# First column block of the first FFN: input x fetched in four pieces, first weights fetched and split by columns, in a fused two-layer decoder trunk on Trainium2

## What is computed

```
def swiglu(x, w_gate, w_up, w_down):
    return (jax.nn.silu(x @ w_gate) * (x @ w_up)) @ w_down
...
    for l in range(DEPTH):
        x = layer_norm(ALPHA * x + 0.5 * swiglu(x, ffn1_w_gate[l], ffn1_w_up[l], ffn1_w_down[l]),
                       ln1_g[l], ln1_b[l])
        mix = hybrid_mixer(x, w_in[l], ...)
        x = layer_norm(ALPHA * x + mix, ln2_g[l], ln2_b[l])
        x = layer_norm(ALPHA * x + 0.5 * swiglu(x, ffn2_w_gate[l], ffn2_w_up[l], ffn2_w_down[l]),
                       ln3_g[l], ln3_b[l])
```

## Time and profile before

| | |
|---|---|
| median of 3 runs | 1083.84 us (1083.62 to 1085.15) |
| the profiled execution's own time | 1083.67 us |
| its span, first to last instruction | 1081.9 us |
| PE busy | 1072.1 us, 99% of the span |
| PE weight loads busy | 882.7 us, 82% |
| DVE / ACT / GpSimd (POOL) busy | 772.0 / 579.4 / 137.3 us |
| mean DMA rate over the span | 209 GB/s |
| granted TensorE clock, mean | 0.999 |

### The profile page before, as it was taken

The page is one execution under the profiler, slowest core; times in us unless marked ns, Lnnn a source line. Parts: engine busy times, 40 slices in busy tenths (PEclk is TensorE's granted clock), DMA queues, the critical chain, the costliest instruction groups (busy, mean ns, idle before and its releaser), DMA issues.

```text
span 1081.9 us, 14282 instructions
## 1 busy us (share of the span) xinstructions
PE 1072.1 (99%) x5197; PEld 882.7 (82%) x5197; DVE 772.0 (71%) x779; ACT 579.4 (54%) x641; POOL 137.3 (13%) x137
## 2 busy tenths in 40 slices
PE   8999999999999999999999999999999999999997
PEld 6888888888888788888888888888878887888886
DVE  5756557799979775555679665677999787655566
ACT  5755654768554544444456655547774546344441
POOL 1498000000000000000006970000000000000000
PEclk9999999999999999999999999999999999999999
DMA  8877879355566486777737877775455674688761
GB/s 285 263 216 231 296 223 225 105 184 171 175 185 208 149 272 226 233 259 225 250 124 231 248 244 254 230 199 165 148 166 157 195 268 133 209 268 270 235 208 40
DMA packets 192371, 226.39 MB, mean 209 GB/s; under 512 B 31540, under 2 KB 157128, under 8 KB 192328
## 3 DMA queue, kind: packets, MB, share of 16 engines
q1 hardware_dynamic: 192328, 225.83, 65.5%
HBM read 214.26 MB, written 11.53 MB: 209 GB/s over the span
## 4 chain that ended last, share of the span: by engine, by line
PE 97%; DMA 1%; SPq 1%; DVE 1%; issue 0%; ACT 0%; DVEq 0%
PE ps L578 25%; PE ps L555 19%; PE ps L557 18%; PE ps L556 18%; PE ps L538 4%; PE ps L540 2%; PE ps L974 1%; PE ps L976 1%; PE ps L975 1%; PE ps L593 1%; DMA raw<-in_ffn_w_up 1%; PE ps L901 1%; DMA tp<-in_ln_b 0%; PE ps L686 0%; PE ps L685 0%; PE ps L684 0%
## 5 line engine op out<-in xcount | busy, mean ns | idle before, releaser
L1449 DVE TENSOR_TENSOR w_lo<-raw,w_hi 128x2048 fp32r<-128x2048 f32 x172 | 399.9, 2329 | 166.7 <-ACT w_hi L1058 165.6
L1058 ACT CAST w_hi<-raw 128x2048 fp32r<-128x2048 f32 x172 | 328.1, 1910 | 162.1 <-PE ps L578 78.9
L555 PE MATMUL ps<-w_hi,xT 128*128 128x512 f32 x848 | 331.8, 391 | 0.3 <-DVE w_lo L1461 0.2
L556 PE MATMUL ps<-w_lo,xT 128*128 128x512 f32 x848 | 330.1, 389 | 0.0
L557 PE MATMUL ps<-w_hi,xT 128*128 128x512 f32 x848 | 330.1, 389 | 0.0
L555 PEld LDWEIGHTS ps<-w_hi,xT 128*128 128x128 f32 x848 | 159.2, 188 | 36.2 <-issue 2.5
L557 PEld LDWEIGHTS ps<-w_hi,xT 128*128 128x128 f32 x848 | 159.2, 188 | 33.0
L556 PEld LDWEIGHTS ps<-w_lo,xT 128*128 128x128 f32 x848 | 159.2, 188 | 32.7
L578 PE MATMUL ps<-w_hi,rows_hi 128*128 128x512 f32 x396 | 126.6, 393 | 0.0
L578 PE MATMUL ps<-w_hi,rows_lo 128*128 128x512 f32 x396 | 125.4, 390 | 0.0
L578 PE MATMUL ps<-w_lo,rows_hi 128*128 128x512 f32 x396 | 125.2, 389 | 0.0
(11 more groups left out here) (248 smaller groups left out, 1117.1 us busy)
## 6 DMA issues: line engine op xcount, KB each, us to landing
raw<-in_ffn_w_down SPq DMA_DIRECT2D x44, 1024.0 KB, 6.6
raw<-in_ffn_w_gate SPq DMA_DIRECT2D x86, 512.0 KB, 4.1
raw<-in_ffn_w_up SPq DMA_DIRECT2D x86, 512.0 KB, 5.2
raw<-in_w_in SPq DMA_DIRECT2D x30, 1024.0 KB, 5.1
hid_dram<-qT SPq DMA_DIRECT2D x160, 64.0 KB, 2.8
qT<-hid_dram SPq DMA_DIRECT2D x40, 256.0 KB, 2.6
raw<-in_w_out SPq DMA_DIRECT2D x8, 1024.0 KB, 4.9
raw<-in_w_in SPq DMA_DIRECT2D x8, 512.0 KB, 5.0
```

What stands on the lines that cost most here:

```text
L555: mm(o, xT[:, c, 0, tok], h, start=c == UPPER_FIRST[0], stop=False, skip_group_check=True)
L556: mm(o, xT[:, c, 0, tok], w, start=False, stop=False, skip_group_check=True)
L1058: nc.scalar.copy(w_hi[s][:, :], raw[s][:, :]).then_inc(hi_made.sem, 1)
L1449: tt(w_lo[s][:, :], raw[s][:, :], f32(w_hi[s][:, :]), ALU.subtract).then_inc(lo_made.sem, 1)
```

## The change

x comes in four pieces by pairs of columns: columns 4 and 5 for each tile by itself (128 KB each), then the pairs (6, 7), (0, 1) and (2, 3) for both tiles (256 KB each). The weights of columns 4, 5 and 6 are issued by ACT, one column and matrix at a time (six transfers of 128 KB), column 7 by SP in the same way, columns 0, 1 and 2, 3 by SP as pairs (256 KB each). Casts and subtractions of the first weights are done one column (512 wide) at a time. PE takes the products column by column for both tiles, turns the next pair of x two columns ahead of its use, and starts with the two high products of column 4 before any low part exists. One block of zero products of 6 is cut to 5, one of 3 to 1, one of 2 to 1.

```
-            load_upper(0)
-            for dst, src in first_columns_of(4, 2, 0):
-                sp.dma_start(dst, src).then_inc(first_landed, 16)
-            load_upper(1)
+            load_rows(0)
+            load_rows(1)
...
-                    load(l, k0, lambda r: first_columns_of(6, 2, 0))
-                    sp.dma_start(xtok[:, :, 0:D // 2], x[0].rearrange("(t p) d -> p t d", p=P)[:, :, 0:D // 2]
-                                 ).then_inc(x_lower, 16)
-                    for dst, src in first_columns_of(0, 2, 1):
-                        sp.dma_start(dst, src).then_inc(second_landed, 16)
-                    load(l, k0 + 1, lambda r: first_columns_of(2, 2, 1))
+                    load_pair(1)
+                    load(l, k0, lambda r: first_column(7))
+                    load_pair(2)
+                    load_columns(0)
+                    load_pair(3)
+                    load(l, k0 + 1, lambda r: first_columns_of(2))
```

PE:

```
                 pe.wait_ge(zero_made, 1)
-                zeros(6)
+                zeros(5)
                 pe.wait_ge(ident_made, 1)
...
+                turn_rows(0)
+                zeros(1)
+                turn_rows(1)
+                zeros(1)
+                pe.wait_ge(first_hi, 1)
+                high_products(0)
+                high_products(1)
+                turn_pair(1)
+                pe.wait_ge(first_lo, 1)
+                low_products(0)
+                low_products(1)
+                pe.wait_ge(first_lo, 2)
+                both_tiles(5)
+                turn_pair(2)
                 pe.wait_ge(x_lo.sem, 4)
...
+                both_tiles(6)
+                take(0, 0)
+                both_tiles(7).then_inc(used.sem, 1)
+                turn_pair(3)
+                pe.wait_ge(x_lo.sem, 6)
+                pe.wait_ge(first_lo, 4)
+                both_tiles(0)
                 pe.wait_ge(second_lo.sem, second_lo.at(0, 0))
...
+                both_tiles(1)
+                pe.wait_ge(x_lo.sem, 8)
+                pe.wait_ge(first_lo, 5)
+                both_tiles(2)
+                take(0, 1)
+                both_tiles(3).then_inc(used.sem, 1)
```

ACT (DVE follows the same order with the low parts):

```
+                for c in (4, 5, 6):
+                    for dst, src in first_column(c):
+                        nc.scalar.dma_start(dst, src).then_inc(column_landed[c], 16)
                 sc_.wait_ge(zero_made, 1)
                 act_(warm[:, :], zero_b[:, 0:1], ACT.Silu)
...
+                rows_hi_(0)
+                column_hi(4, first_hi, column_landed[4], 32)
+                rows_hi_(1)
+                column_hi(5, first_hi, column_landed[5], 32)
+                pair_hi(1)
+                column_hi(6, first_hi, column_landed[6], 32)
+                column_hi(7, hi_made.sem, landed[0], LANDED[0])
+                pair_hi(2)
+                column_hi(0, first_hi, column_landed[0], 32)
+                column_hi(1, second_hi.sem, column_landed[0], 32)
+                pair_hi(3)
+                column_hi(2, first_hi, landed[1], LANDED[1])
+                column_hi(3, hi_made.sem, landed[1], LANDED[1])
```

More of the change, by code:

```diff
@@ L236, in trunk @@
         xn_made = Events(sem("xn_made"), 3 * 4)
-        tp_made = Events(sem("tp_made"), 3 * NT, before=NT)
+        tp_made = Events(sem("tp_made"), 3 * NT, before=3)
         tp_upper = Events(sem("tp_upper"), 3 * NT, before=NT)
@@ new lines, in turn_pair, with both_tiles @@
+                def turn_pair(p):
+                    pe.wait_ge(x_pair[p], 16)
+                    for n, c in enumerate(PAIRS[p]):
+                        for t in range(NT):
+                            at = n * SEQ + t * P
+                            last = nc.tensor.transpose(ps[:, (0, 6, 4, 7)[p], at:at + P], xtok[:, t, c * P:c * P + P],
+                                                       ident[:, :])
+                    last.then_inc(tp_made.sem, 1)
+                def both_tiles(c):
+                    hi, lo = (first_w_hi, first_w_lo) if c > 3 else (w_hi[0], w_lo[0])
+                    for t in range(NT):
+                        last = gate_up(hi, lo, t, c, t)
+                    return last
@@ L1709, in turn_input @@
-                low(0, 1, 2)
-                for c in range(2):
-                    dve.wait_ge(first_hi, c + 1)
-                    low_first(c).then_inc(first_lo, 1)
-                low(1, 1, 4)
-                dve.wait_ge(hi_made.sem, hi_made.at(0, 1))
-                low_first(2).then_inc(first_lo, 1)
-                low_first(3).then_inc(lo_made.sem, 1)
-                low(0, 0, 6)
-                low(1, 0, 8)
-                second = rest_halves(0, 0)
-                second(0)
@@ new lines, in column_lo @@
+                def column_lo(c, made, n, then):
+                    dve.wait_ge(made, n)
+                    hi, lo = (first_w_hi, first_w_lo) if c > 3 else (w_hi[0], w_lo[0])
+                    tt(paired(lo)[:, c % 4, :], paired(raw[c < 4])[:, c % 4, :], f32(paired(hi)[:, c % 4, :]),
+                       ALU.subtract).then_inc(then, 1)
+                rows_lo_(0)
+                column_lo(4, first_hi, 1, first_lo)
+                rows_lo_(1)
+                column_lo(5, first_hi, 2, first_lo)
```

136 lines of the change are left out of this document (65 added, 71 removed).

## The result

The changed kernel took 1085.65 us (median of 22 runs, 1083.91 to 1089.97), the kernel before it 1083.89 (22 runs beside them, 1082.89 to 1085.76). The ratio is 1.0015, with a 95% interval of 1.0009 to 1.0021. So it is slower, by less than the 0.2% I took as the bound, and 0.45 us above the top of my range. The profiled execution took 1085.63 with a span of 1083.8; before it was 1083.67 and 1081.9. The traces therefore have 1.9 us to explain; the medians differ by 1.8.

What follows compares the result with a forecast made beforehand. PE, busy 1072.1 of 1081.9 us, was taken as the bound, with chunk 3 held by the small rows' DMA. The head's 1.2 us gain is all waited away there: change 0.0, forecast 1083.7, range 1082.3 to 1085.2.

Steps and rivals of the forecast that it cites:

- The head: PE's first block, up to chunk 2: claimed to end at 19.0 instead of 20.23, a gain of 1.2 us.
- the +0.65 for smaller pieces: First 1.5 MB of loads: smaller transfers might run at 273 instead of 308 GB/s, shifting everything behind by 0.65 us.
- my scale of megabytes: Head's data: arrival times read from megabytes landed in the earlier trace, putting pair 1 and column 5 at about 6.3.
- That quarter costs nothing.: SP's issue of `w_down`: a quarter of a microsecond later (16.1), claimed free because the queue is full then.
- chunk 5 is issued when chunk 2's low part is made (20.0, unchanged): Step on SP's chunk 5 issue, used to bound what gain could pass the down product at 0.9 us.
- 26.11, change 0.0: PE's start on chunk 3: held by the small rows' unchanged arrival at 23.45, so the head's gain is waited away.
- the second wait: Down product at 31.68 needs `rows_lo`, ready at 30.75 and hanging on the read-back; at most 0.9 us can pass.
- behind 26.11 the whole run shows no further wait of PE: Reading of the earlier profile: after chunk 3 PE never waits, so the end comes a fixed time after 26.11.
- The early small rows: Rival at chunk 3: small rows land earlier and up to 0.9 us passes, 1082.8; chance 0.3.
- a faster head by two queues: Rival in the head: 348 instead of 308 GB/s, all data 1.2 us sooner, at most -1.7, 1082.0; chance 0.06.
- ACT's issues: Rival in the head: at 1.37 each ACT is free at 10.4 and chunk 3 is 3.5 later, 1087.2; chance 0.07.
- The clock: Rival at PE's first weights: eight products at the lower clock level cost 1.6 us, net +0.2, 1083.9; chance 0.07.

Runs made afterwards that it cites:

- i1: The changed kernel with three more zero products: six instead of five at the start, two between column 4's first products and pair 1; ratio 1.0017.
- j1: i1 with one more wait on SP ahead of the hidden writes, for ACT's fifth cast; ratio 1.0007.
- e1: The changed kernel with each of the 7 zero products cut into four of a quarter's width; ratio 1.0008.
- f1: The changed kernel with the first five zero products cut into eighths and the other two into quarters; ratio 1.0003.
- e2: The kernel before without its last five zero products; ratio 1.0000.
- g1: The kernel before with its eleven zero products in 6 pairs of instructions instead of 11, wide float32 zeros replacing narrow ones; ratio 0.9998.
- h1: The changed kernel with one more wait on SP ahead of the hidden writes, for ACT's fifth cast; ratio 1.0020.
- e3: The changed kernel with the six transfers of columns 4 to 6 issued by SP instead of ACT, one queue only; ratio 1.0017.
- h2: The changed kernel with columns 2 and 3 ahead of pair 3 and the small rows behind chunk 3, measured again; ratio 1.0002.
- f2: The changed kernel with casts and subtractions of columns 2 and 3 ahead of those of pair 3; ratio 0.9997.
- f3: The changed kernel with DVE's copies of the small rows and PE's turns of them moved behind chunk 3; ratio 1.0009.

## Why the prediction was wrong

**What held.** ACT's six issues took 0.41 to 0.46 (I had 0.47 with the gap), its first cast came at 5.01 (5.0), the first weights at 5.94 (6.05). PE did wait for DVE before chunk 3, DVE for the small rows, and these came at 23.62 (23.45): chunk 3 at 26.28 (26.11). That the head's gain stops there was right. That the rows came only 0.17 later was in part luck: `w_down` went out 1.0 later than before, and in i1, where it went out 0.26 earlier than in the changed kernel, they came 0.20 later (23.82).

**The head** gained 0.73 and not 1.2. The transfers were no slower than I took them (322 GB/s from 3 to 9 us, 308), so the +0.65 for smaller pieces at the top of my range didn't show either. But column 5 was there at 7.45, where my scale of megabytes had 6.3. Its two transfers were ACT's third and fourth, issued at 1.67 and 2.16; my scale knew only one queue's order, which is my reading and not tested. PE waited 0.76 for its low part, pair 3 was turned at 13.59, column 3's low part was ready at 16.85 (16.1). So `w_down` went out at 16.95.

**"That quarter costs nothing."** It became 1.0 us (16.95 against 15.94), and it did cost a little: SP then was still at its small rows until 20.16 (19.74 + 0.42) when chunk 2's low part was ready (19.66), and chunk 5 went out 0.37 later. This contradicts the step "chunk 5 is issued when chunk 2's low part is made (20.0, unchanged)": I had not counted the seven issues that stand between as a limit on SP.

**The step that failed** is the one behind "26.11, change 0.0": the sum has no term after chunk 3, because the read-back of 26.73 was left where it was. I had worked out the second wait (the down product at 31.68 needs `rows_lo`, ready at 30.75) and a margin of 0.9, and used it only to bound a gain. The read-back depends on the writes, on chunk 5 ahead of them, and on what SP meets while issuing. It came 2.63 later (29.36). Of this 0.37 is chunk 5's later issue and 2.26 the longer way from there (8.76 against 6.50). Against its margin the down product lost 1.80: chunk 3's 0.17, and 1.47 of waiting, and the rest small. With 6.50 the read-back would be at 27.1, and `rows_lo` (3.33 behind it to its start before, 0.69 long) at 31.1; PE without its wait would be there at 32.01 (33.48 - 1.47). So by this estimate the wait is gone without the fetch and 0.33 of the 1.80 remains. i1 and j1 show the first half of it: 1.2 us of wait, gone with the writes held back. They don't show the second: j1's down product began at 32.80, still 1.1 later than before, since its `w_down` (17.22) and its small rows (24.53) were later than the changed kernel's.

**A reading of mine that was too short.** I wrote that behind 26.11 the whole run shows no further wait of PE. The products have none, but the earlier trace rows covers only 25 to 60 us, and the weight loads of the kernel before wait later too, ten times and 3.3 us in all, for DVE's `xtok` (L593). The profiles differ before 33.5 us, so this changed nothing here.

**Why the change brought it about.** Nothing in the diff touches the hidden writes. But the head's gain brought them 0.73 forward (21.79), and the fetch went from 21.1 to 21.6, with a head of fewer PE instructions. Before, nearly all of the fetch (21.1 to 22.2) fell into a gap of SP, between 21.19 (20.73 + 0.46) and 22.52. It is shown that the meeting costs. That the number of instructions on PE moves the fetch is shown for added ones (e1 and f1, 3 us earlier, though f1 added twice as many as e1); with fewer it went 2.7 us later in e2, whose head was late itself, and 0.5 us earlier in g1. How often it happens in executions without a profile can't be seen.

**The rivals.** The early small rows and a faster head by two queues didn't come; ACT's issues weren't slow. The clock rose in time in the profiled execution (products 0.23 apart from 7.2 on), and late in others with the changed head (h1, e3, f1, h2). I had priced it at 0.2 through PE alone; through pair 3 and `w_down` it moved chunk 3 to 28.98 in h1. No rival of mine had the read-back *later*, which was the missing case on the slow side.

## What to carry to other kernels

A wait that is worked out as a bound on a gain is also the place where a loss shows: ask what could make it later, and how little that may be (here 0.9 us). After moving work, look at which DMA issues of the queue engine now stand beside instruction fetches, and compare the duration of the issue and the landing of its neighbours with those before. And where a transpose or a cast for the fast engine stands ahead of the work that frees a buffer, put it behind: f2 did this by moving two lines and undid the loss, though the fetch had moved out of the way as well.

## What I had not expected of the hardware

- Between 16 and 27 us an issue of SP took 0.25 to 0.50 us, but 1.35 (e1, f1), 1.57 (g1), 1.60 (the changed kernel) or 1.75 (i1) where one 16 KB packet of instructions was fetched at that moment. If it was a hidden write, the 512 KB load issued before it landed after 6.7 to 7.6 us instead of 5.0 to 6.0. A fetch during the same transfer with no issue beside it cost nothing (j1, 5.4).
- This is no rule for the whole program. Over the whole trace of the kernel before, 20 of SP's 548 issues overlap a fetch and only 4 of them took over 0.8 us, while 14 issues over 0.8 us overlap none (one of `w_in`, for example, took 1.14 at 181.8).
- Holding a write back by 3 us made the read behind it start 1.6 us earlier.
- TensorE took its higher level of 2.4 GHz at 7.2 in one execution and only behind 12 weight products in another of the same head (h1), after an idle 0.62 us ahead of pair 1 (f1 and h2 rose late without such a wait). After 2.42 us of waiting in f3 products ran at the 1.2 GHz level again (0.43 each, granted clock 0.57).
